# The value projection of a gated linear attention layer, computed inside its loop of groups

## The reference, cut to what matters

```python
def _mixer_gla(h, w_in, gate_w2, gate_b, norm_g, w_out):   # h: 256 tokens x 1024
    proj = h @ w_in
    q = heads(proj[..., :512], 128) * 128 ** -0.5           # 4 heads
    k = heads(proj[..., 512:1024], 128)
    v = heads(proj[..., 1024:2048], 256)                    # "b_v": 4 blocks of 256 columns
    r = proj[..., 2048:3072]                                # "b_r": the output gates
    gl = proj[..., 3072:].reshape(bn, s, 2, 16)
    gate_logit = einsum(gl, gate_w2) + gate_b
    log_a = log_sigmoid(gate_logit) / 16                    # forward and backward
    o = gla(q, k, v, log_a[0]) + flip(gla(flip(q), flip(k), flip(v), flip(log_a[1])))
    o = rmsnorm(o, norm_g) * silu(r)
    return o @ w_out                                        # "b_out"
```

## Time and profile before

| | |
|---|---|
| median of 3 runs | 1563.91 us (1560.41 to 1564.23) |
| the profiled execution: device time | 1569.33 us |
| its span in the trace | 1567.6 us |
| PE busy | 91% of the span |
| DVE, ACT, POOL busy | 64%, 49%, 26% |
| chain that ended last, share of PE | 72% |
| mean granted clock of PE | 0.959 of full speed |
| `b_v` in the trace | 1209.0 to 1235.2 us |
| `b_r` | 1235.2 to 1258.1 us |
| loop of 16 groups, and what follows up to `b_out` | 1258.1 to 1321.6 us |

### The profile page before, as it was taken

The page is one execution under the profiler, slowest core; times in us unless marked ns, Lnnn a source line. Parts: engine busy times, 40 slices in busy tenths (PEclk is TensorE's granted clock), DMA queues, the critical chain, the costliest instruction groups (busy, mean ns, idle before and its releaser), DMA issues.

```text
span 1567.6 us, 27516 instructions
## 1 busy us (share of the span) xinstructions
PE 1430.1 (91%) x10981; PEld 1376.4 (88%) x10981; DVE 1011.0 (64%) x1726; ACT 773.8 (49%) x1211; POOL 404.8 (26%) x362
## 2 busy tenths in 40 slices
PE   4979999989898999898988889999999987999998
PEld 4979999988898999898878879999997976899997
DVE  6687868657676655579655557865464565876442
ACT  3424465574363433464573545664354643666333
POOL 1566774304300000156372401730005000200000
PEclk9889999999899999989999999999999998999999
DMA  9944553233746745635310005555552510365540
GB/s 354 363 135 148 175 162 108 82 107 120 240 153 221 227 158 161 202 85 159 108 54 1 1 1 161 158 183 171 187 161 83 179 38 14 122 188 189 176 146 28
DMA packets 202480, 223.74 MB, mean 143 GB/s; under 512 B 7608, under 2 KB 197723, under 8 KB 200317
## 3 DMA queue, kind: packets, MB, share of 16 engines
q1 hardware_dynamic: 201072, 220.67, 43.8%
q10 hardware_dynamic: 1293, 1.47, 0.3%
HBM read 221.07 MB, written 1.05 MB: 142 GB/s over the span
## 4 chain that ended last, share of the span: by engine, by line
PE 72%; DVE 13%; ACT 6%; POOL 3%; issue 3%; DMA 2%; SPq 0%; DVEq 0%; ACTq 0%; POOLq 0%
PE acc L596 18%; PE acc L598 17%; PE acc L597 17%; DVE GB L1828 2%; DVE wlo L473 1%; ACT whi L463 1%; POOL H L967 1%; PE acc L537 1%; PE acc L530 1%; DMA raw<-in_w_ffn_in 1%; DVE SQX L940 1%; DMA XIN<-in_x 1%; PE acc L531 1%; POOL AM L1194 1%; PE pm L2359 1%
## 5 line engine op out<-in xcount | busy, mean ns | idle before, releaser
L596 PE MATMUL acc<-HH,whi 128*128 128x256 f32 x1744 | 501.2, 287 | 29.1 <-issue 9.1
L463 ACT ACTIVATE whi<-raw 128x1024 fp32r<-128x1024 f32 (+2 forms) x380 | 378.7, 1029 | 242.1 <-PE acc L598 194.1
L597 PE MATMUL acc<-HL,whi 128*128 128x256 f32 x1744 | 496.0, 284 | 0.0
L598 PE MATMUL acc<-HH,wlo 128*128 128x256 f32 x1744 | 495.9, 284 | 0.0
L473 DVE TENSOR_TENSOR wlo<-raw,whi 128x1024 fp32r<-128x1024 f32 (+2 forms) x292 | 340.0, 1196 | 208.5 <-ACT whi L463 205.8
L596 PEld LDWEIGHTS acc<-HH,whi 128*128 128x128 f32 x1744 | 334.4, 192 | 36.6 <-issue 28.6
L597 PEld LDWEIGHTS acc<-HL,whi 128*128 128x128 f32 x1744 | 334.0, 192 | 0.3 <-issue 0.2
L598 PEld LDWEIGHTS acc<-HH,wlo 128*128 128x128 f32 x1744 | 333.6, 191 | 0.0
L473 POOL TENSOR_TENSOR wlo<-raw,whi 128x1024 fp32r<-128x1024 f32 x88 | 213.6, 2446 | 397.9 <-DVE wlo L473 246.6
L596 PE MATMUL acc<-HIDH,whi 128*128 128x256 f32 x688 | 195.7, 284 | 6.4 <-ACT whi L463 4.5
L597 PE MATMUL acc<-HIDL,whi 128*128 128x256 f32 x688 | 195.4, 284 | 0.0
(11 more groups left out here) (554 smaller groups left out, 2541.7 us busy)
## 6 DMA issues: line engine op xcount, KB each, us to landing
raw<-in_mlp_w SPq DMA_DIRECT2D x64, 1024.0 KB, 5.3
raw<-in_w_in SPq DMA_DIRECT2D x36, 1024.0 KB, 5.3
raw<-in_w_ffn_in SPq DMA_DIRECT2D x22, 1024.0 KB, 5.3
raw<-in_a_w_in SPq DMA_DIRECT2D x16, 1024.0 KB, 5.7
raw<-in_b_w_in SPq DMA_DIRECT2D x12, 1024.0 KB, 5.3
raw<-in_w_ada_mix SPq DMA_DIRECT2D x8, 1024.0 KB, 7.1
ADR<-in_w_ada_ffn SPq DMA_DIRECT2D x8, 1024.0 KB, 11.5
raw<-in_w_ssm_out SPq DMA_DIRECT2D x8, 1024.0 KB, 5.2
```

The lines of the kernel that those rows point to most:

```text
L463: act.activation(whi[:, (s.t0 + 2 * u + h) % 4, 0:k], raw[:, place(s, b, u) % 4, 0:k, h * P:h * P + P], ACT.Copy).then_inc(hi_ready, 1)
L596: pe.matmul(acc[:, q, 0:T], whi[:, slot, i], hh, start=first and i == 0, stop=False)
L597: pe.matmul(acc[:, q, 0:T], whi[:, slot, i], hl, start=False, stop=False)
L598: m = pe.matmul(acc[:, q, 0:T], wlo[:, slot, i], hh, start=False, stop=final and i == k - 1)
```

## The change

`b_r` goes ahead of `b_v`. `b_v` is no longer a section: its block 0 is computed right after `b_r` (two tiles, into `pm` bank 0), and the tiles of block h + 1 at the ends of groups 4h + 1 and 4h + 3 of the loop (into `pm` bank 3). Its splits go to fixed places in the queues of ACT and DVE, and so does the split of the first block of `b_out`. ACT evacuates a block in one operation, for block h > 0 in group 4h, behind its exps. The eight halves of `b_r` are evacuated as plain copies, and one silu runs over all of them. The sums for the norm move to `pm` bank 2, so `head_std` runs once per head and `values(h)` waits for `head_std(h - 1)`. The gate logits are now worked on beside `b_r`. The tile-by-tokens branch (`tok_major`) is gone from the section code.

```diff
         Section("b_qk", cols(b_in, 0), 4),
+        Section("b_r", cols(b_in, B_R), 4),
         Section("b_v", cols(b_in, B_V), 4),
-        Section("b_r", cols(b_in, B_R), 4),
...
@@ ACT
-            def b_v(b, u, h, j):
+            def b_v(b):
                 tile_done(act, SEC["b_v"], b, 1)
-                act.activation(VT2[:, h, ds(b * COLS, COLS)], acc[:, out_slot(SEC["b_v"], u, h), 0:T], ACT.Copy)\
-                   .then_inc(acc_free, 1)
+                act.activation(VT2[:, :, b * COLS:b * COLS + COLS],
+                               pm[:, 3 if b else 0].rearrange("p (k c) -> p k c", k=NT), ACT.Copy).then_inc(acc_free, 2)
...
-            split_section(act, split_hi, SEC["b_v"], b_v, extra=v_more)
-            split_section(act, split_hi, SEC["b_r"], table_evac(SEC["b_r"], RG, ACT.Silu))
+            split_section(act, split_hi, SEC["b_r"], table_evac(SEC["b_r"], RG, ACT.Copy), extra=r_more)
+            act.preload_act_table_set("silu_and_others")
+            act.wait_ge(acc_free, SEC["b_r"].o0 + 4 + 8)
+            act.activation(RG[:], RG[:], ACT.Silu)
+            for h in range(2):
+                split_hi(act, SEC["b_v"], 1, 1, h)
...
-                act.wait_ge(l2_sum, 2 * i + 2)
-                inv_sqrt(act, RS[:, 2 * i:2 * i + 2], pm[:, 3].rearrange("p (e t) -> p e t", e=2), T, 0, l2_std)
+                act.wait_ge(l2_sum, i + 1)
+                inv_sqrt(act, RS[:, i], pm[:, 2, 0:T], T, 0, l2_std)
...
             act.preload_act_table_set("natural_log_exp_and_others")
+            b_v(0)
             for g in range(4 * B_HEADS):
...
-                elif h == 2 and p == 3:
-                    head_std(0)
+                elif h and p == 3:
+                    head_std(h - 1)
                 elif h == 3 and p == 2:
                     heads_hi(0)
+                if h and p == 0:
+                    b_v(h)
+                if g in (0, 4, 8):
+                    nxt = SEC["b_v"] if g < 8 else SEC["b_out"]
+                    for i in range(2):
+                        split_hi(act, nxt, (g // 4 + 2) % 4, (g // 4 + 2) % 4, i)
             head_copy(3)
-            head_std(1)
+            head_std(3)
@@ DVE
-            split_section(v, split_lo, SEC["b_v"], None, extra=v_more)
             split_section(v, split_lo, SEC["b_r"], None, extra=r_more)
+            for h in range(2):
+                split_lo(v, SEC["b_v"], 1, 1, h)
...
+                if g % 4 in (1, 2) and g < 12:
+                    nxt = SEC["b_v"] if g < 8 else SEC["b_out"]
+                    split_lo(v, nxt, (g // 4 + 2) % 4, (g // 4 + 2) % 4, g % 4 - 1)
@@ PE
-            pe_section(pe, SEC["b_v"], hrhs, tok_major=True)
             pe_section(pe, SEC["b_r"], hrhs)
+
+            def value_tile(b, tk):
+
+                s = SEC["b_v"]
+                if tk == 0:
+                    pe.wait_ge(hi_ready, 2 * b + s.t0 + 2)
+                    pe.wait_ge(raw_used, 2 * (b + s.w0) + 2)
+                    if b > 1:
+                        pe.wait_ge(acc_free, 2 * b + s.o0 + 4)
+                o_ = pm[:, 3 if b else 0, tk * T:tk * T + T]
+                tc, slot = slice(tk * P, tk * P + P), (s.t0 + 2 * b) % 4
+                for i in range(KT):
+                    w_hi, w_lo = whi[:, slot:slot + 2, i], wlo[:, slot:slot + 2, i]
+                    pe.matmul(o_, HH[:, i, tc], w_hi, start=i == 0, stop=False)
+                    pe.matmul(o_, HL[:, i, tc], w_hi, start=False, stop=False)
+                    m = pe.matmul(o_, HH[:, i, tc], w_lo, start=False, stop=i == KT - 1)
+                if tk == 1:
+                    m.then_inc(w_used, 2)
+            pe.wait_ge(la_ok, 1)
+            for tk in range(NT):
+                value_tile(0, tk)
...
             pe.wait_ge(ll_ok, 4)
             pe.wait_ge(w_ok, 1)
-            pe.wait_ge(acc_free, SEC["b_out"].o0 + 4)
+            pe.wait_ge(acc_free, SEC["b_v"].o0 + 4)
             exponents(0)
             exponents(1)
+            pe.wait_ge(la_ok, 4)
+            pe.wait_ge(acc_free, SEC["b_v"].o0 + 4 + 2)
...
                 elif h and p == 2:
                     value_sums(h - 1)
+                if h < 3 and p % 2:
+                    value_tile(h + 1, p // 2)
```

More of the change, by code:

```diff
@@ L538, in pe_first, with pe_section @@
                 m.then_inc(w_used, 1)
-        def pe_section(pe, s, rhs, tok_major=False, free=None, ready=None, after=None):
+        def pe_section(pe, s, rhs, free=None, ready=None, after=None):
             if s.name not in NORM_OF:
                 pe.wait_ge(acc_free, s.o0 + 4)
-            block_ = pe_block(pe, s, rhs, tok_major, free, ready)
+            block_ = pe_block(pe, s, rhs, free, ready)
             def body(b, u, last, j):
@@ L549, in pe_section, with pe_block @@
             over_blocks(pe, s, body)
-        def pe_block(pe, s, rhs, tok_major=False, free=None, ready=None):
+        def pe_block(pe, s, rhs, free=None, ready=None):
             def body(b, u, last, j, only=(0, 1)):
@@ L578, in body @@
                     slot, q = (s.t0 + 2 * u + h) % 4, out_slot(s, u, h)
[L579 to L598, removed]
+                    for i in range(k):
+                        hh, hl = rhs(k0 + i)
+                        pe.matmul(acc[:, q, 0:T], whi[:, slot, i], hh, start=first and i == 0, stop=False)
+                        pe.matmul(acc[:, q, 0:T], whi[:, slot, i], hl, start=False, stop=False)
+                        m = pe.matmul(acc[:, q, 0:T], wlo[:, slot, i], hh, start=False, stop=final and i == k - 1)
                     m.then_inc(w_used, 1)
@@ L1608, in qk_more, with r_more @@
                     log_gate(0)
-            def v_more(b):
+            def r_more(b):
                 if b:
@@ L2212, in gate_lo, with r_more @@
                 v.tensor_tensor(LAL[:, q], LA[:, q], LAH[:, q].bitcast(F32), ALU.subtract).then_inc(ll_ok, 1)
-            def v_more(b):
+            def r_more(b):
                 gate_log(b)
[L2216 to L2221, removed]
+                if b:
+                    gate_lo(b - 1)
+                if b == 3:
+                    gate_lo(3)
             split_section(v, split_lo, SEC["b_qk"], None)
-            split_section(v, split_lo, SEC["b_v"], None, extra=v_more)
             split_section(v, split_lo, SEC["b_r"], None, extra=r_more)
+            for h in range(2):
+                split_lo(v, SEC["b_v"], 1, 1, h)
             def half_of(ap):
@@ L2282, in normed @@
                 c.wait()
-                v.wait_ge(l2_std, i + 1)
+                v.wait_ge(l2_std, 2 * i + 2)
                 h4 = H[:, 4 * i:4 * i + 4].rearrange("p (h e) t -> p h e t", e=2)
@@ L2722, in values @@
                 pe.wait_ge(s_ok, 9 * h + 9)
+                pe.wait_ge(acc_free, SEC["b_v"].o0 + 4 + 2 * h + 2)
                 if h:
+                    pe.wait_ge(l2_std, h)
                     pe.wait_ge(bo_ok, h)
@@ L2733, in value_sums @@
                 pe.wait_ge(bo_ok, h + 1)
-                if h == 2:
-                    pe.wait_ge(l2_std, 1)
                 for e in range(2):
-                    m = pe.matmul(pm[:, 3, h % 2 * T:h % 2 * T + T], ones, SQX[:, 2 * h + e], start=e == 0, stop=e == 1)
+                    m = pe.matmul(pm[:, 2, 0:T], ones, SQX[:, 2 * h + e], start=e == 0, stop=e == 1)
                 m.then_inc(l2_sum, 1)
```

## The result

| | median | ratio to the kernel before, 95% interval |
|---|---|---|
| before | 1564.0 us (1560.4 to 1565.3) | |
| changed kernel | 1577.8 us (1561.3 to 1580.7) | 1.0061 [1.0033, 1.0089] |
| the same pair in a second group of runs | 1572.9 us against 1564.7 | 1.0053 [1.0021, 1.0086] |

The change makes the kernel slower by 0.2 to 0.9%, 8 to 14 us by the medians. (One run of 1985 us, at a mean clock of 0.648, is left out of the changed kernel's median and of all comparisons.) The profiled execution has a span of 1576.4 us and a time of 1578.1.

What follows compares the result with a forecast made beforehand. PE, busy for 91% of the span, was taken as the bound; the parts summed to -0.8 us at full clock, plus 3.0 for the clock gave +2.2: 1563.9 + 2.2 = 1566.1 us, range 1557.5 to 1571.

Steps and rivals of the forecast that it cites:

- `b_r` in `b_v`'s place: Section `b_r`: each weight half waits only for its own split, so `b_v`'s restarts go; -3.3 us.
- Start of the loop: Between `b_r` and head 0's third score product: silu and its table load now in series; +3.5 us.
- Head 0 from there on: Head 0 after its third score product: tiles cover small DVE waits and two split halves; -1.0 us.
- Fronts: Starts of heads 1 to 3: ACT's copy and splits delay exps; +2.95 us each in 1 and 2, +1.0 in 3.
- Heads 1 and 2: Rest of both heads: one tile covered, -1.7 us each; head 2's own earlier loss gone, -3.1, less the clock.
- Tail: End of the loop: `head_std(3)` works on 256 instead of 512 columns, twice; -0.4 us.
- The sum of -0.8 us at full clock: Whole change: all seven parts added, before any price for half clock; -0.8 us.
- the walk: The part-by-part reckoning of PE, ACT and DVE queues through `b_r`, loop and tail; -0.8 us at full clock.
- the clock: Idle stretches at starts of heads 0, 1 and 2 bring half clock, 1.5 us each; two of three, +3.0.
- The forecast of +2.2: Whole kernel: full-clock sum plus two slow-clock stretches; +2.2 us, chance 0.60.
- Rival B: Head starts: exps of 4h + 1 behind tile, copy and splits cost more; +6.2 us, chance 0.26.

Runs made afterwards that it cites:

- e3: Changed kernel without the silu over the gates and the table load ahead of it; 1569.4 us, 1.0033 to the kernel before.
- e1: Changed kernel with 6, 9, 9 and 4 useless matmuls ahead of the third score product of heads 0 to 3; 1560.3 us, 0.9990 to the kernel before.
- e0: Changed kernel run again, unchanged, as the reference of the second group; 1572.9 us, 1.0053 to the kernel before.
- e2: Changed kernel with ACT's value-block copy and two weight splits moved behind the exps of group 4h + 1; 1551.6 us, 0.9922 to the kernel before.
- e6: e2 with the splits of value block 1 behind group 1's exps and the copy of block 0 behind group 0's; 1551.7 us, 0.9900.
- e8: e6 with four unused matmuls ahead of `b_out`; 1553.6 us, 0.9924 to the kernel before.
- e7: Changed kernel with only the two weight splits moved behind the exps of group 4h + 1; 1564.2 us, 0.9990 to the kernel before.

## Why the prediction was wrong

By the points of the prediction:

1. *`b_r` in `b_v`'s place*: right. 23.0 us for its 192 matmuls, no restart.
2. *Start of the loop*: right. Third product 14.06 us after the gate section, predicted 14.5. The price of the silu in it was too high: taking it out gave 1.5 us (e3), because the copy of block 0 waits for the tiles anyway. No drain showed behind the table loads: the first, of 1.28 us, began at 1230.93 and the silu at 1232.23.
3. *Head 0 from there on*: 12.9 us predicted, 12.75 measured at full clock (17.72 - 4.97 in e1).
4. *Fronts*: third products predicted at 5.1, 5.1 and 3.15 us, measured at 5.06, 5.06 and 3.17.
5. and 6. *Heads 1 and 2*: 21.2 us predicted, 21.14 measured at full clock (e1). Head 3 comes to 18.5 + 1.0 = 19.5 by the prediction and took 21.07 in e1; the 1.6 us more are the low clock at its last `values`.
7. *Tail*: `head_std` takes two operations of 0.47 and 0.42 us instead of 0.69 and 0.63, so -0.4 as predicted.

The sum of -0.8 us at full clock is borne out by e1. Up to `b_out` the walk has -0.4 us; e1's trace takes 113.1 us from the section after `b_qk`, 0.5 more than the kernel before, with that one low stretch of 1.6 us in it.

The step that failed is **the clock**: "Each such stretch costs up to 1.7, I take 1.5. Which of them get one is open: two of three, +3.0." The mechanism was right and its size was off, in three ways.

First, too few gaps were counted. In both traces all four brought the low clock, head 3 with its 2.1 us too, which I had counted out, and once more came at the last `values`. The trace of the kernel before already spoke against counting long gaps only. It has the same wait of 1.62 us in heads 1, 2 and 3, and behind two of the three the clock fell: in head 2 the stretch of the earlier trace rows, and in head 3 a second one of 3.6 us at 0.53 (1313.4 to 1317.0), which the prediction didn't see:

```profile
1294.78 0.68 PE L2717 MATMUL pm<-KQ 128*128 128x128 f32 x4 [1.62 <-DVE SS L2268]
1312.02 0.68 PE L2717 MATMUL pm<-KQ 128*128 128x128 f32 x4 [1.62 <-DVE SS L2268]
1314.00:1316.00 2.00, 2.00 (x8) 1.73 (x7) 2.00 (x6) 0.00 (x0) 0.00 (x0) 0.50 0.00 0
```

Second, the stretch was taken for 3.4 us from a gap of 2.9; behind gaps of 4.0 it was nearly twice as long, with its beginning in the gap itself. The gap's length alone doesn't set it: behind the same wait of 2.85 us in head 0 the clock was low for some 3.4 us in the first trace (0.72 over 6.0 us) and for more than 5.5 in e0's (0.52 over 5.8). Third, it falls on `values` and `exponents`, on which head copy, exps and DVE wait, so nothing of it is hidden.

Per head that is 2.5, 2.7, 2.7 and 1.3 us (e0 against e1), 9.2 in the loop, 10 by the ratios and 12.6 between the medians, where I had 3.0. The forecast of +2.2 hung on that one term. Rival B named the right place and the right sign, and its sign came true (heads of 23 us and more). But its +6.2 held 4.5 us for the clock, and the other 2.5, a later start of the loop and a dearer part 1, did not come; 8 to 14 us came. To let all three gaps count, as the Trainium skill has it ("TensorE: Matmul & The Clock Gate", the section on HAM oscillation), gave +3.7: nearer than my two of three, and still less than half of what came.

## What to carry to other kernels

When work is moved into a loop on PE, what ACT and DVE do for it must stand behind the operations that the next step of PE needs, even if these look early: here one copy and two splits, placed behind two exps instead of ahead of them, were worth 21 us. Price an idle stretch of PE as gap plus low clock: a gap of 4 us cost another 2.7 us behind it, one of 2.9 us 1.5 to 2.5, and one of 2 us 1.3 to 1.6 us or nothing. Filling a gap with useless matmuls is a cheap test that parts the two, and was itself worth 10 to 12.6 us.

## What was not expected of the hardware

One program on one core had executions 18 us apart (1561.6 to 1579.6) with the same instructions, split by the mean granted clock (0.961 to 0.964 against 0.951 to 0.958); a median of three such runs can miss by more than the change that is measured. The kernel before had runs from 1551.9 to 1569.5 in the same group, again roughly in the order of their clocks (0.970 down to 0.959). The gaps at the head starts don't explain the spread alone. e2, without them, stayed within 4.1 us (1550.9 to 1555.0), but e6 and e8, which have none in heads 1 to 3 either, spread over 7.5 and 8.7 us, as much as e7 with its gaps of 2.2 us (7.7). Which gaps brought the low clock in an execution that was not traced stays open.
